# Second mixer and first loads: weight units rounded and subtracted at other times

## The reference, cut to what matters

```
qkv = (xn @ w_qkv).reshape(b, s, 3, SB_HEADS, SB_HEAD_DIM)
q = rms_norm(qkv[:, :, 0], q_gain); k = rms_norm(qkv[:, :, 1], k_gain); v = qkv[:, :, 2]
z = einsum('bhqd,bhkd->bhqk', q, k) * scale          # per block of 128 queries
log_1m = where(s < t, log_sigmoid(-z), 0)
w = where(s < t, exp(log_sigmoid(z) + sum of log_1m behind s), 0)
o = einsum('bhqk,bhkd->bhqd', w, v);  x = x + o @ w_o
```

## Time and profile before

| | us |
|---|---|
| median of 3 runs | 2148.38 (2148.08 to 2148.53) |
| the profiled execution's own time | 2146.76 |
| its span, first to last instruction | 2145.0 |
| PE busy | 2105.5 (98%) |
| DVE busy | 806.8 (38%) |
| ACT busy | 770.2 (36%) |
| POOL busy | 862.6 (40%) |

### The profile page before, as it was taken

One profiled execution on the slowest core, in us unless ns is written; L12 is line 12 of the kernel. 1 busy time (PEld: TensorE's weight loads), 2 busy tenths in 40 slices (PEclk: granted clock), 3 DMA queues, 4 the chain that ended last, 5 costly groups with the idle time before them and its releaser, 6 DMA issues. The chain is left out here.

```text
span 2145.0 us, 26797 instructions
## 1 busy us (share of the span) xinstructions
PE 2105.5 (98%) x9710; PEld 1700.8 (79%) x9710; DVE 806.8 (38%) x1227; ACT 770.2 (36%) x1058; POOL 862.6 (40%) x364
## 2 busy tenths in 40 slices
PE   7999999999999999999999999999999999999999
PEld 6888888677777888888888888888777778888887
DVE  5222211657853432222216222212778764222200
ACT  5222232344344442223323222223656644222221
POOL 3444444333322444444454444544222234444443
PEclk9999999999999999999999999999999999999999
DMA  4222323321221322322232222323111122222332
GB/s 162 98 98 98 100 96 118 120 74 65 70 69 59 98 98 98 98 98 98 98 117 80 96 98 98 108 98 108 40 60 50 59 71 92 94 97 98 108 108 78
DMA packets 56573, 196.84 MB, mean 92 GB/s; under 512 B 6400, under 2 KB 7296, under 8 KB 56512
## 3 DMA queue, kind: packets, MB, share of 16 engines
q1 hardware_dynamic: 55248, 193.25, 27.2%
q10 hardware_dynamic: 1264, 2.75, 0.4%
HBM read 193.75 MB, written 2.10 MB: 91 GB/s over the span
## 5 line engine op out<-in xcount | busy, mean ns | idle before, releaser
L371 POOL TENSOR_TENSOR w_lo<-raw,w_hi 128x1024 fp32r<-128x1024 f32 x360 | 862.3, 2408 | 1263.8 <-ACT w_hi L804 1262.8
L397 PE MATMUL ps<-xn_hi,w_hi 128*128 128x512 f32 x1912 | 758.8, 397 | 8.7 <-DVE xn_lo L1113 8.5
L399 PE MATMUL ps<-xn_hi,w_lo 128*128 128x512 f32 x1912 | 748.6, 392 | 0.0
L398 PE MATMUL ps<-xn_lo,w_hi 128*128 128x512 f32 x1912 | 748.5, 391 | 0.0
L397 PEld LDWEIGHTS ps<-xn_hi,w_hi 128*128 128x128 f32 x1912 | 362.0, 189 | 91.1 <-POOL w_lo L371 9.0
L804 ACT ACTIVATE w_hi<-raw 128x1024 fp32r<-128x1024 f32 x360 | 366.9, 1048 | 159.2 <-PE ps L399 119.9
L399 PEld LDWEIGHTS ps<-xn_hi,w_lo 128*128 128x128 f32 x1912 | 361.4, 189 | 76.9
L398 PEld LDWEIGHTS ps<-xn_lo,w_hi 128*128 128x128 f32 x1912 | 361.9, 189 | 74.6 <-issue 1.2
L1081 DVE TENSOR_TENSOR scratch<-ps,rstd 128x512 f32<-128x512 f32 x200 | 137.8, 690 | 580.7 <-PE ps L399 580.2
L397 PE MATMUL ps<-h_hi,w_hi 128*128 128x512 f32 x704 | 273.9, 389 | 0.0
L398 PE MATMUL ps<-h_lo,w_hi 128*128 128x512 f32 x704 | 273.9, 389 | 0.0
(11 more groups left out here) (180 smaller groups left out, 1490.3 us busy)
## 6 DMA issues: line engine op xcount, KB each, us to landing
raw<-weights SPq DMA_DIRECT2D x360, 512.0 KB, 3.4
x_sb<-x_t SPq DMA_DIRECT2D x8, 256.0 KB, 6.0
bias<-rel ACTq DMA_DIRECT2D x1, 2048.0 KB, 10.2
out_t<-x_sb SPq DMA_DIRECT2D x8, 256.0 KB, 4.4
rope<-ropes ACTq DMA_DIRECT2D x1, 512.0 KB, 3.6
const<-consts SPq DMA_DIRECT2D x1, 128.0 KB, 6.8
ki<-ki ACTq DMA_DIRECT2D x1, 128.0 KB, 2.2
to_round<-consts SPq DMA_DIRECT2D x1, 64.0 KB, 6.8
```

The source lines that it names most:

```text
L371: nc.gpsimd.tensor_tensor(w_lo[s][:, :, :], raw[s][:, :, :], w_hi[s][:, :, :].bitcast(F32), ALU.subtract).then_inc(S["lo_done"], 1)
L397: pe.matmul(to, w_hi[s][:, k, :], hi, start=opens, stop=False)
L398: pe.matmul(to, w_hi[s][:, k, :], lo, start=False, stop=False)
L399: last = pe.matmul(to, w_lo[s][:, k, :], hi, start=False, stop=ends)
```

## The change

1. Second mixer, ACT: in the even head nothing is rounded beside DVE's subtraction any more; the even head rounds unit 3t+6 behind its last Exp, the odd head 3t+7 beside and 3t+8 behind. Unit 5 is rounded ahead of the heads.
2. Second mixer, POOL: its loop is written out there, and the remainder of unit 3t+6 waits until both norms of pair t+1 are done (`qk_split` at 2t+4).
3. Second mixer, ahead of the heads: the mean square of the first k moves two tiles later on PE, the fills of `goes_on` (L1434, L1437) ahead of the reciprocal on DVE.
4. Start: unit 1 is loaded behind all of x; ACT rounds it behind x, unit 2 between the fourth and fifth square, and unit 4 ahead of the root; the remainders of units 0 to 3 are made by DVE, and POOL begins with unit 4; PE's mean square stands behind the fourth tile of unit 2 in place of the first.

A buffer `zeros`, a number `WARM` and a semaphore are declared and not used.

```diff
-BESIDE = [[3 * (h // 2) + (7 if h % 2 else 5)] for h in range(SB_HEADS - 2)] + [[27], [30]]
-BEHIND = [[] if h % 2 else [3 * (h // 2) + 6] for h in range(SB_HEADS - 3)] + [[26], [28, 29], [31]]
+BESIDE = [[3 * (h // 2) + 7] if h % 2 else [] for h in range(SB_HEADS - 2)] + [[27], [30]]
+BEHIND = [[3 * (h // 2) + (8 if h % 2 else 6)] for h in range(SB_HEADS - 2)] + [[28, 29], [31]]
+AFTER_NORMS = [3 * t + 6 for t in range(PAIRS - 1)]
...
         for k in range(DT):
             sp.dma_start(X[:, k, :], x[:, k, :]).then_inc(x_landed[k], 16)
-            if k == 5:
-                load(1, 1)
+        load(1, 1)
         load(2, 2)
...
-        with pool.Fori(0, UNITS // NSLOT) as it:
+        pool.wait_ge(S["lo_done"], NSLOT)
+        with pool.Fori(1, U_QKV // NSLOT) as it:
+            for s in range(NSLOT):
+                rest(it, s)
+        for u in range(U_QKV // NSLOT * NSLOT, U_FFN4):
+            n = u - U_QKV
+            if n in AFTER_NORMS:
+                pool.wait_ge(S["qk_split"], 2 * AFTER_NORMS.index(n) + 4)
+            rest(u // NSLOT, u % NSLOT)
+        with pool.Fori(U_FFN4 // NSLOT, UNITS // NSLOT) as it:
...
             def first_mean(k):
-                if k == 1:
+                if k == 4:
...
             project(0, 2 * UK + 3)
             head_mean_square(0, 0)
-            project(2 * UK + 3, 2 * UK + 5)
+            project(2 * UK + 3, 2 * UK + 7)
             head_mean_square(0, 1)
-            project(2 * UK + 5, LEAD)
+            project(2 * UK + 7, LEAD)
...
                 if first:
-                    ahead(u)
-                    if n == 0:
+                    if n:
+                        ahead(u)
+                    else:
                         ahead(u + 1)
+                        ahead(u + 2)
                     root_mean_square(FFN_STAT[n])
...
             head_square(1, 0)
+            round_unit(5)
             for h in range(SB_HEADS):
...
+        act.wait_ge(S["gains_in"], 16)
         for k in range(DT):
             act.wait_ge(x_landed[k], 16)
-            if k == 0:
-                act.wait_ge(S["gains_in"], 16)
             round_input(k, T_START)
-            if k == 5:
-                round_weights(1, 1, 0)
+        round_weights(1, 1, 0)
         for k in range(DT):
+            if k == 4:
+                round_weights(2, 2, 0)
             first_square(k)
...
+        def first_rest(u):
+            dve.wait_ge(S["hi_done"], u + 1)
+            nc.vector.tensor_tensor(w_lo[u][:, :, :], raw[u][:, :, :], w_hi[u][:, :, :].bitcast(F32), ALU.subtract)\
+                .then_inc(S["lo_done"], 1)
+
+        first_rest(0)
         dve.wait_ge(S["gains_in"], 16)
         for k in range(DT):
             split_input(k, T_START)
+        first_rest(1)
         for k in range(DT):
+            if k == 4:
+                first_rest(2)
             add_square(k, first_squares[:, k, :], S_START)
+        first_rest(3)
```

More of the change, by code:

```diff
@@ L38 @@
 NSLOT = 4
+WARM = 16
 AHEAD = 2
@@ L204, in build @@
     to_round = place("to_round", [P, P], F32, at)
+    zeros = place("zeros", [P, TOK], BF16, at)
     at = [region]
@@ L264, in build @@
     names = """hi_done lo_done unit_done consts_in to_round_in gains_in head_gains_in rope_in bias_in cols_ready
-        x_updated x_normed sq_done ssq_zeroed ssq_done ms_done rms_done rstd_ready
+        x_updated x_normed sq_done zeros_made ssq_zeroed ssq_done ms_done rms_done rstd_ready
         sq2_done ssq2_zeroed ssq2_done ms2_done r1_made m2_scaled rms2_done r2_made
@@ L861, in tile @@
                 elif u is not None:
-                    ahead(u)
+                    if u > 2:
+                        ahead(u)
                     ahead(u + 1)
@@ L1429, in update_from @@
                 return U_QKV + (AT_AGAIN if k == 3 else OUT_AT[4] if k < 3 else OUT_AT[k]) + 1
-            reciprocal_rms(S_FFN3)
-            dve.wait_ge(S["cols_ready"], 3)
-            make(0, 0)
             nc.vector.memset(goes_on[:, :], 1.0).then_inc(S["goes_on_made"], 1)
@@ L1438, in mixer_2 @@
                     .then_inc(S["goes_on_made"], 1)
+            reciprocal_rms(S_FFN3)
+            dve.wait_ge(S["cols_ready"], 3)
+            make(0, 0)
             make(0, 1)
@@ L1444, in mixer_2 @@
             make(1, 0)
+            split_squares(1, 0)
             zero_ssq(S_MIX2)
@@ L1449, in mixer_2 @@
                 more = t + 1 < PAIRS
-                if not odd and more:
-                    split_squares(t + 1, 0)
                 if h:
@@ L1477, in mixer_2 @@
                     make(t + 2, 0)
+                    split_squares(t + 2, 0)
                 elif more:
```

## The result

| | before | after |
|---|---|---|
| median of the runs | 2148.23 us (2146.12 to 2148.53, 4 runs) | 2117.57 us (2116.53 to 2118.04, 4 runs) |
| profiled execution, span | 2146.76 us, 2145.0 us | 2117.63 us, 2115.8 us |
| mean granted clock | 0.995 | 0.998 |

The ratio is 0.9859, with an interval of 0.9842 to 0.9876: the change makes the kernel faster, by 30.7 us between the medians. The forecast was 2122.2 with a range from 2118.5.

The account below looks back on a forecast made before the run. PE, busy 98% of the span, was taken as the bound, so its idle and low-clock time could be won. 16.3 + 6.2 + 3.7 = 26.2 us off 2148.4 gave 2122.2 us, 8-in-10 range 2118.5 to 2129.

Parts of the forecast that it names:

- the seven waits and their cause: Second mixer: PE's waits at L638 for `scratch` vanish once POOL's remainders no longer hold off DVE's norms; 16.3 us.
- 16.3 us: Second mixer: PE's idle time in seven waits of `turn_values` for DVE's `scratch`, all forecast to be won.
- the clock behind these waits: Second mixer, odd halves: four falls of PE's clock behind the L638 waits go too, 6.2 us; bounds nothing to 6.2.
- a POOL remainder runs beside each: Second mixer, L1411: all 15 average 1.49 us beside POOL, so DVE instructions reading PSUM are not slowed.
- PE's first matmul waits for x, not for weights: the 8.5 us stay: Kernel start: PE's wait ahead of the first matmul was forecast to remain unchanged at 8.5 us.
- the start, 3.7 us: Kernel start: 0.35 us up to unit 1 plus 3.3 from the vanished `ssq` wait; bounds 3.2 to 3.9.
- the median of the runs is 1.6 above it: Base of the sum: the median lies 1.6 us above the profiled execution's 2146.76, so 2148.4 was used.
- ACT's idle time ahead of its Abs: Second mixer: of 1.63 us idle on ACT, some 0.3 are left, so the Abs is not late.
- The `k_sq_lo` wait: Head 0: PE's first wait for `k_sq_lo`, 2.9 us, stays, and so does the low clock behind it.
- The slack at unit 1: Kernel start: PE comes to unit 1 at 16.8, 1.7 us behind its remainder, done by 15.1.
- the slower case: Second mixer: POOL stands at the norms and PE waits for unit 3t+6; 2158 at 9 us late, 3 in 100.
- a rival's mechanism: Second mixer: POOL holds off DVE's two-input SBUF instructions such as the scan; new-collision rival, 2131 to 2139, 9 in 100.

Follow-up runs that it names:

- e5_no_norm_wait: The changed kernel without POOL's wait for the norms, roundings left where the change has them: 2126.42 us, ratio 0.9906.
- e6_old_roundings: The changed kernel with ACT's second-mixer roundings back at their old places, POOL's wait for the norms kept: 2120.37 us, ratio 0.9877.
- e2_start_only: The changed kernel with the second mixer's part undone and the start's parts kept: 2138.53 us, ratio 0.9966.
- e4_before_again: The kernel before, unchanged line for line, run as if it were a new one: 2146.28 us, ratio 0.9999.
- e12_change_again: The changed kernel itself, repeated without edits as base for other runs: 2117.27 us, ratio 0.9862.
- e9_head0_tiles: The changed kernel with four projection tiles between head 0's mean squares and scores, two moved from head 1: 2113.25 us, ratio 0.9844.

## Why the prediction was right, and where it was wrong

**Right: the seven waits and their cause.** They are gone, the norms last 0.74 and 0.43, and the two halves of the collision come back one by one in e5_no_norm_wait and e6_old_roundings. The Trainium skill, "SBUF — State Buffer", section "Who interferes with whom", has the rule; the traces agree for the scale (2.94 beside POOL, 0.74 alone) and for the scan (5.02, 2.82).

**Mis-sized: their price, "16.3 us".** It is the sum of PE's idle times. From the scores of the odd head to `turn_values` it took 8.86 us before and takes 6.19 now, and from there to the next scores 7.43 (where the clock held) and now 7.38:

```profile
1553.97:1562.83 8.86, 6.35 (x39) 5.23 (x38) 8.72 (x9) 5.22 (x5) 3.67 (x2) 1.00 0.37 118
```

So 2.67 + 0.05 = 2.72 a pair for a gap of 2.51; with the first pair's shorter wait (7.57 - 6.19 + 0.05 = 1.43) it makes 6 x 2.72 + 1.43 = 17.8, which is 1.5 more than 16.3. The 0.2 beside each gap is independent of its length: in e5_no_norm_wait a gap of 1.29 costs 7.64 - 6.19 + 0.05 = 1.50, and in e6_old_roundings one of 0.43 costs 14.19 - 13.57 = 0.62 to 0.63. PE is booked as busy for it (6.35 against 6.19 above).

**Right: "the clock behind these waits", 6.2 us.** No odd half has a fall now. 17.8 + 6.2 = 24.0 is what the traces give for the mixer. The 6.2 belong to the profiled execution of before, with its four falls; in e2_start_only's, with two, they are 2.8.

**Thin: "a POOL remainder runs beside each" of L1411.** ACT's rounding begins when L1411 does, so POOL overlaps only the last 0.35 of its 1.49 us. That PSUM readers aren't held off was thus hardly shown before. The change shows it: the copy of 1.49 us at 1550.91 lies wholly beside POOL's 1550.74 to 1553.16.

**Wrong: "PE's first matmul waits for x, not for weights: the 8.5 us stay".** That sentence was read off the name of the releaser, `xn_lo`, without a look at why `xn_lo` was late. POOL's remainder of unit 0 held it in all traces with it (first matmul at 8.45, 8.46 and 8.48 whether x came early or late) and in none without (7.4 to 7.9). It is the same collision that was found in the mixer. Its price is 1.0 us where x lands early (8.46 against 7.48). In the profiled execution of before x was late: without POOL `xn_lo` would have ended at 7.23 + 0.75 = 7.98, so of the 0.96 between the two profiled executions some 0.3 are the collision and the rest is x's landing, which is luck.

**Mis-sized: the start, 3.7 us for 5.3.** Up to unit 1's first matmul PE is 1.50 earlier (15.69 against 17.19) where 0.35 was forecast: 0.96 from the first matmul, 0.35 at tiles 6 and 7, and 0.2 because one matmul fewer runs at the lower level (the first of 0.39 us is at 13.15, before at 14.52). From there into unit 3 it is 3.4 (12.01 us for 15.39), as forecast. The last 0.4 is a wait that the forecast doesn't name, for unit 4. POOL and PE before, and POOL in the change:

```profile
35.64 4.77 POOL L371 TENSOR_TENSOR w_lo<-raw,w_hi 128x1024 fp32r<-128x1024 f32 x2 [11.31 <-ACT w_hi L804]
...
38.10 0.50 PE L397 MATMUL ps<-xn_hi,w_hi 128*128 128x512 f32 x1
```
```profile
23.70 2.38 POOL L373 TENSOR_TENSOR w_lo<-raw,w_hi 128x1024 fp32r<-128x1024 f32 x1 [23.25 <-DVE w_lo L1512]
```

Before, ACT rounded unit 4 behind the root and POOL's remainder was ready at about 38.0; PE, whose matmuls are 0.23 apart, went from 37.57 to 38.10 and took 0.34 for the next step. The change rounds unit 4 ahead of the root, and its remainder is there 7 us before PE is. The estimate of 1.2 us for a DVE remainder was right (1.23), `ssq` was done at 22.2 for a forecast of 21.5, and the mean square found it ready at 23.85. The eight additions took 6.1 us in place of 5.2.

**Wrong: "the median of the runs is 1.6 above it", added as a constant.** The terms were read in one execution, and the median of before is another draw from runs that lie 6.3 us apart (e4_before_again); nothing says that the distance of the two stays. After the change the median and the profiled execution agree within 0.1. Against the medians of before in the three later sets (2146.25 to 2147.97) the change's own medians are 28.7 to 30.7 lower. The sum by the profiled execution, 2120.6, was the better base.

The three together make the miss: 1.5 (stalls) + 1.6 (start) + 1.5 (base) = 4.6, and 2122.2 - 2117.57 is 4.6. The range ended too early below, because idle time was taken for the upper bound of what a wait can cost, and the first wait had no bound but nothing.

**The rest, point by point.** ACT's idle time ahead of its Abs is 0.16 us for a forecast of 0.3: not late. The `k_sq_lo` wait stayed, as forecast, and e9_head0_tiles shows that it was an order of tiles and no fate. The slack at unit 1 was 0.6 us in the profiled execution of the change (15.69, and the remainder done at 15.12) and nothing in e12_change_again, where 1.7 were forecast: PE came 1.1 sooner than the forecast had it. POOL waiting at the norms delays no unit that PE needs; the slower case would have needed much more.

## What to carry to other kernels

Look in a trace for DVE instructions with two SBUF inputs, or casts between SBUF tiles, that are longer than their like and end where POOL's end: move POOL's work beside DVE instructions that read PSUM, and ask of every wait for such a tile, the first one of the kernel too, whether POOL made it late. Price a wait of PE from start to start and not by its idle time. If the kernel before spreads widely from run to run, its clock is a term of the sum: take the profiled execution as the base, and expect the spread to shrink with the waits. Before two traces are compared, see whether the clock fell at the same places in both: one fall is 1.3 to 1.6 us here, more than some effects that were looked for.

## What the hardware showed that was not expected

- DVE's scan with two SBUF inputs, until then only a rival's mechanism, is held off as a whole by POOL: 5.02 us for 2.82, with a POOL instruction of 2.37.
- A stall of PE costs about 0.2 us beside its idle time, for gaps of 0.43, 1.29 and 2.51 us alike (0.63, 1.50 and 2.72).
- A wait of 2.1 to 3.3 us is followed by a fall to the lower clock level in some executions and not in others. Behind six waits of 2.5 us each there are 4, 4 and 2 falls in three traces, 1.3 to 1.6 us apiece. Over all fourteen traces, 8 of 14 waits for `qi` (2.13 to 2.17 us) and 10 of 12 for `k_sq_lo` (2.94) have one, and 2 of 4 for `ssq` at the start (3.12 to 3.25). Behind the waits of 1.3 us and less in `turn_values` no fall was seen.
- The rise to the upper level at the start is as uneven: the first matmul of 0.4 us is at 14.52 in one trace of the kernel before and at 11.60 in the other, though PE starts at 8.45 and 8.48. The Trainium skill, "TensorE: Matmul & The Clock Gate", section "What's actually happening", says that the number of matmuls at the lower level varies between runs of one kernel; these two traces agree.
